# The sticks' values tiles spread over the first attention steps, the gate tiles moved back by three steps

## What is computed

```python
def second_block(x, ...):
    h = rms_norm_2(x, mix_norm_gain)
    proj = h @ w_in
    q_a, k_a, v_a, q_b, k_b, v_b, gate_logits = jnp.split(proj, SPLIT_POINTS, axis=-1)
    y_a = sliding_window_sink_attention(q_a, k_a, v_a, q_gain, k_gain, sinks)   # "windows"
    y_b = stick_breaking_attention(q_b, k_b, v_b)                               # "sticks"
    gates = jax.nn.sigmoid(gate_logits + gate_bias).reshape(b, s, 2, d)
    merged = gates[:, :, 0] * (y_a @ w_up_swa) + gates[:, :, 1] * (y_b @ w_up_sb)
    x = x + merged @ w_out
    h = rms_norm_2(x, ffn_norm_gain)
    return x + peer_ffn(h, peer_w_q, peer_sub_keys, peer_u, peer_v)

def stick_breaking_attention(q, k, v):   # 8 heads of 64, causal, blocks of 128 queries
    z = (q @ k.T) * dh ** -0.5
    log_beta = log_sigmoid(z)
    log_keep = where(before, log_sigmoid(-z), 0)
    suffix = cumsum(log_keep, reverse=True) - log_keep
    return where(before, exp(log_beta + suffix), 0) @ v
```

## Time and profile before

| | us |
|---|---|
| median of 3 runs | 2158.72 |
| lowest and highest of them | 2151.64, 2168.53 |
| the profiled execution, its time | 2159.31 |
| its span | 2158.0 |
| mean granted clock of TensorE in it | 0.985 of full |

### The profile page before, as it was taken

How to read it: one execution, slowest core, us unless ns; L and a number is a source line. 1 busy time by engine, 2 the same in 40 slices (tenths; PEclk the granted TensorE clock), 3 DMA queues, 4 the chain that set the end, 5 groups by cost and what they waited for, 6 DMA issues and landing times.

```text
span 2158.0 us, 36392 instructions
## 1 busy us (share of the span) xinstructions
PE 2096.6 (97%) x14838; PEld 1895.6 (88%) x14838; DVE 1460.1 (68%) x2450; ACT 1054.1 (49%) x1589; POOL 185.8 (9%) x102
## 2 busy tenths in 40 slices
PE   8999999999999999889999899999999999999999
PEld 7997789899889998579988678999999998888887
DVE  5655784766566665856645676899899995555555
ACT  5444633254455444645444875545544445444443
POOL 0000013300010000110004003243000000000000
PEclk9999998999999999899999899999999999999999
DMA  5556221256655555236556335556544446666664
GB/s 199 186 190 209 82 95 60 73 182 195 195 176 177 187 190 182 80 119 196 195 185 203 101 98 188 169 163 187 176 147 147 148 148 195 194 190 191 195 188 153
DMA packets 97637, 352.62 MB, mean 163 GB/s; under 512 B 10896, under 2 KB 12688, under 8 KB 97088
## 3 DMA queue, kind: packets, MB, share of 16 engines
q1 hardware_dynamic: 97472, 350.29, 51.0%
HBM read 349.20 MB, written 1.05 MB: 162 GB/s over the span
## 4 chain that ended last, share of the span: by engine, by line
PE 86%; DVE 8%; ACT 3%; issue 1%; POOL 1%; DMA 0%; SPq 0%; ACTq 0%; DVEq 0%
PE psum L276 26%; PE psum L278 25%; PE psum L277 25%; PE psum L2711 2%; DVE tile_low L205 2%; PE psum L851 1%; ACT tile_high L193 1%; PE psum L347 1%; POOL small L1667 1%; PE psum L1049 1%; PE psum L929 1%; DVE peer_active L2918 0%; ACT hT L490 0%; PE psum L472 0%; PE psum L769 0%
## 5 line engine op out<-in xcount | busy, mean ns | idle before, releaser
L205 DVE TENSOR_TENSOR tile_low<-raw_tiles,tile_high 128x1024 fp32r<-128x1024 f32 x598 | 738.6, 1237 | 508.5 <-ACT tile_high L193 508.2
L193 ACT ACTIVATE tile_high<-raw_tiles 128x1024 fp32r<-128x1024 f32 x642 | 678.2, 1058 | 712.9 <-PE psum L278 708.3
L276 PE MATMUL psum<-hT,tile_high 128*128 128x256 f32 x2560 | 723.5, 283 | 8.8 <-issue 4.7
L277 PE MATMUL psum<-hT,tile_high 128*128 128x256 f32 x2560 | 715.5, 279 | 0.0
L278 PE MATMUL psum<-hT,tile_low 128*128 128x256 f32 x2560 | 715.3, 279 | 0.0
L276 PEld LDWEIGHTS psum<-hT,tile_high 128*128 128x128 f32 x2560 | 486.8, 190 | 10.9 <-issue 7.8
L277 PEld LDWEIGHTS psum<-hT,tile_high 128*128 128x128 f32 x2560 | 484.3, 189 | 0.1
L278 PEld LDWEIGHTS psum<-hT,tile_low 128*128 128x128 f32 x2560 | 483.4, 189 | 0.0
L276 PE MATMUL psum<-tile_high,hT 128*128 128x512 f32 (+1 forms) x816 | 326.1, 400 | 3.3 <-DVE hT L2060 1.6
L278 PE MATMUL psum<-tile_high,hT 128*128 128x512 f32 (+1 forms) x816 | 320.8, 393 | 0.0
L277 PE MATMUL psum<-tile_low,hT 128*128 128x512 f32 (+1 forms) x816 | 318.9, 391 | 0.0
(11 more groups left out here) (357 smaller groups left out, 2226.2 us busy)
## 6 DMA issues: line engine op xcount, KB each, us to landing
raw_tiles<-ffn_in_dram SPq DMA_DIRECT2D x176, 512.0 KB, 3.5
raw_tiles<-peer_u_dram SPq DMA_DIRECT2D x128, 512.0 KB, 3.5
raw_tiles<-peer_v_dram SPq DMA_DIRECT2D x128, 512.0 KB, 3.5
raw_tiles<-ffn_out_dram SPq DMA_DIRECT2D x88, 512.0 KB, 4.3
raw_tiles<-w_kv_dram SPq DMA_DIRECT2D x16, 512.0 KB, 4.2
raw_tiles<-in_gates_dram SPq DMA_DIRECT2D x16, 512.0 KB, 3.5
raw_tiles<-peer_q_dram SPq DMA_DIRECT2D x16, 512.0 KB, 3.8
raw_tiles<-w_k_dram SPq DMA_DIRECT2D x8, 512.0 KB, 3.6
```

What stands on the lines that cost most here:

```text
L193: scalar.activation(k.high[:, n % SLOTS, :], k.raw[:, n % RAW_SLOTS, :], ACT.Copy).then_inc(*k.tile_high_made.mark(n))
L205: vector.tensor_tensor(k.low[:, n % SLOTS, :], k.raw[:, n % RAW_SLOTS, :], k.high[:, n % SLOTS, :].bitcast(F32), ALU.subtract).then_inc(*k ...
L276: k.tensor.matmul(out, still[0], moving[0], start=first, stop=False)
L277: k.tensor.matmul(out, still[0], moving[1], start=False, stop=False)
```

## The change

The values of the sticks become woven tiles like the gates'. Two of their four tiles go ahead of step 0, one each into steps 0 and 1, all into banks 0 and 1. ACT copies their sums at step 2, the first gate group waits for that copy, and PE waits for the emptied banks 0 and 1 ahead of the first values' tile. The gate tiles move to steps 3 to 21 without 7, 12 and 17, the bias to steps 7, 12, 17 and 22. The sticks' turning stays in step 18. The order of the tiles in the stream is the same.

```diff
-GATE_STEPS = [step for step in range(19) if step not in (3, 8, 13)]
+VALUES_AHEAD = 2
+VALUE_STEPS = [0, 1]
+GATE_STEPS = [step for step in range(3, 22) if step not in (7, 12, 17)]
+WOVEN_STEPS = VALUE_STEPS + GATE_STEPS
 BIASED_STEPS = [GATE_STEPS[4 * g + 3] + 1 for g in range(4)]
-STICKS_OUT = GATE_STEPS[-1]
+STICKS_OUT = 18
+MIX2_STEPS = BIASED_STEPS[3] + 1
+def woven_tile(step):
+    return FIRST["in_v_b"][0] + VALUES_AHEAD + WOVEN_STEPS.index(step)
...
-    tensor_tokens(k, "in_v_b", k.hT, k.tokens_copied)
+    def woven(i):
+        g, c0 = i // 4 - 1, 2 * (i % 4)
+        n, pair = take(k)
+        pair = tuple(t.rearrange("p (k n) -> p k n", k=2) for t in pair)
+        for tb in range(TB):
+            if c0 == 0 and g == 0:
+                tensor.wait_ge(*k.tokens_copied.at(("in_v_b", tb, 0)))
+            if c0 == 0 and g > 0:
+                tensor.wait_ge(*k.gates_biased.at((tb, g - 1)))
+            for c in range(2):
+                ins = products(k, k.psum[:, tb, :], part(k.hT, EVERY, c0 + c, block(tb)), part(pair, EVERY, c, EVERY),
+                               c0 + c == 0, c0 + c == KC - 1)
+        ins.then_inc(*k.tile_used.mark(n))
     for b in range(2):
         before, key = k.bank_emptied[b]
         tensor.wait_ge(*before.at(key))
     use_banks(k, range(2, 8))
+    for i in range(VALUES_AHEAD):
+        woven(i)
     tensor.wait_ge(*k.qa_made.at(1))
     tensor.wait_ge(*k.ka_made.at(1))
     tensor.wait_ge(*k.features_out.at(("in_qk_b", 1)))
     tensor.wait_ge(*k.ka_made.at(("in_qk_b", 3)))
-    tensor.wait_ge(*k.tokens_copied.at(("in_v_b", 1, 0)))
...
-    for step in range(units + 4):
+    for step in range(MIX2_STEPS):
...
-        if step in GATE_STEPS:
-            gate(GATE_STEPS.index(step))
+        if step in WOVEN_STEPS:
+            woven(VALUES_AHEAD + WOVEN_STEPS.index(step))
...
-    copied("in_v_b", r["v_b"])
+    def values_copied():
+        for tb in range(TB):
+            scalar.wait_ge(*k.tile_used.at(FIRST["in_v_b"][1] - 1))
+            scalar.activation(r["v_b"][:, tb, :], k.psum[:, tb, :], ACT.Copy, scale=root(k, tb)).then_inc(
+                *k.tokens_copied.mark(("in_v_b", tb, 0)))
...
+    split_high(k, FIRST["in_v_b"][0] + VALUES_AHEAD - 1 + SLOTS)
+    for step in range(MIX2_STEPS):
...
-        if step in GATE_STEPS:
-            split_high(k, gates + GATE_STEPS.index(step) + SLOTS)
+        if step == VALUE_STEPS[-1] + 1:
+            values_copied()
+        if step in WOVEN_STEPS:
+            split_high(k, woven_tile(step) + SLOTS)
...
-    split_low(k, FIRST["in_v_b"][1] - 1 + SLOTS)
+    split_low(k, FIRST["in_v_b"][0] + VALUES_AHEAD - 1 + SLOTS)
...
-        if step in GATE_STEPS:
-            split_low(k, gates + GATE_STEPS.index(step) + SLOTS)
+        if step in WOVEN_STEPS:
+            split_low(k, woven_tile(step) + SLOTS)
```

More of the change, by code:

```diff
@@ L2217, in values @@
         v = r["v_b"] if stick else r["kv_a"]
+        if n == 0:
+            tensor.wait_ge(*k.tokens_copied.at(("in_v_b", 1, 0)))
         ps = bank(k, ("values2", n), k.attended, (2, n))
@@ L2227, in values @@
         ins.then_inc(*k.values_done.mark((2, n)))
[L2229 to L2239, removed]
     units = len(MIX2_UNITS)
@@ L2366, in y_high @@
             turned_high(r["y2"][name][0][:, :, block(tb)], (name, tb), k.y2_turned, (name, tb), k.y2_high_made)
-    gates, up = FIRST["in_gates"][0], FIRST["up_sb"][0]
+    up = FIRST["up_sb"][0]
     units = len(MIX2_UNITS)
-    for step in range(units + 5):
+    split_high(k, FIRST["in_v_b"][0] + VALUES_AHEAD - 1 + SLOTS)
+    for step in range(MIX2_STEPS):
         for late in (6, 5, 4, 3, 2):
```

## The result

| | before | changed |
|---|---|---|
| median of 20 runs, us | 2161.05 | 2164.06 |
| lowest to highest, us | 2151.64 to 2168.53 | 2159.40 to 2171.11 |
| span of the profiled execution, us | 2158.0 | 2167.9 |

The ratio is 1.0023 with a 95% interval of 1.0012 to 1.0034: 2.6 to 7.3 us slower. The forecast was 2157.5 us, 1.2 us faster than the 2158.72 known at that time. Both differences are far under the 1% at which the chances were drawn, but the sign was wrong. The slower rival (a loss of 4.2 us) is nearest.

The account below looks back on a forecast made before the run. TensorE's matmul stream was taken to bound the kernel. From values to up projection, 83.9 us work + 15.9 idle + 5.3 half clock = 105.1 against 106.3, a gain of 1.2: 2157.5 us, own range 2153 to 2161, with rivals 2147 to 2166.

Parts of the forecast that it names:

- The slower rival: Values to up projection: clock falls at every pause, four falls, 10.7 us together; loss 4.2 us, 2162 us; chance 0.25.
- Items 1 to 4: Values' first tile to turning of stick 0: idle 0.85 us for banks, 1.15 for the values' copy, 5.2 before the turning.
- Item 5: Steps 5 and 6: DVE saves the bias's 1.41 us and its wait, and TensorE is not held.
- Item 6: Bias in steps 7, 12, 17 without gate tile: TensorE idles 4.7 us, about 1.1 in step 13, 2.6 in 17 and 18.
- Item 7: Behind step 16: five gate tiles instead of three, all TensorE's time; the up projection's first tile follows at once.
- The sum, its term of half clock: Whole stretch: three clock falls, behind steps 4, 8 and 17, at 5.3 us together.
- my two bounds: Cost of one clock fall, read from slow tiles before the change: 1.7 to 4.2 us.
- Its threshold: The slower rival decides once the clock costs more than 6.5 us in the stretch.
- its sign: First scores to up projection: a granted clock below 0.88 would show the slower rival.
- item 4: Turning of stick 0: 5.2 us idle, passed 7.1 us earlier with two tiles (5.7 us) fewer done; only 1.4 us remain.

Follow-up runs that it names:

- the last experiment: The changed kernel with the bias behind the step's vector work and 72 idle matmuls in pauses: stretch 98.89 us, ratio 0.9972 against the kernel before.
- b2: The kernel before with 36 idle matmuls ahead of the turning of stick 0, nothing else: stretch 101.38 us, ratio 0.9983.

## Why the prediction was wrong

Item by item, with the changed kernel's profile moved by the 5.70 us of its later start.

- *Items 1 to 4, the front: right.* The first tile began 0.82 us late (0.85 forecast). The first scores came at 1184.36 (1184.3 forecast), the first gate tile at 1193.45 (1193.0), the turning of stick 0 at 1201.30 (1201.0) behind 4.85 us (5.2). The copy of the values cost 1.40 (1.15).
- *Item 5, steps 5 and 6: right.* There is no pause in them.
- *Item 6, the bias steps: right in place and size of the pauses.* 4.68 us in steps 7 and 8 (4.7), 1.24 in steps 12 and 13 (1.1), 1.96 in 17 and 18 (2.6). The experiment with the bias behind the vector work shows that the order on DVE makes 2.9 us of them; 2.41 us ahead of the turning of stick 4 and the 1.25 of step 13 stay without it.
- *Item 7, the tail: right that it pays in full, with half clock on top.* It takes 10.85 us more, 5.7 for the two tiles; the rest is 1.96 of pause, which item 6 had, and a clock of 0.86 where it was 1.00.
- *The sum, its term of half clock: this is the step that failed.* Idle time was over-estimated by 1.2 us (15.9 for 14.7). Half clock was taken as three falls at 5.3 us together. There were four. From the lengths of the tiles, transposes, scores and values behind each pause I count about 2.6, 2.1, 1.8 and 2.7, together 9.2 us, and 84.2 for the work, against my 83.9. So 105.1 should have been 83.9 + 14.7 + 9.2 = 107.8, and the profiled stretch is 108.2: the up projection's first product came at 1286.0, not near 1283. Of the 3.9 us that were missing, 1.8 are the fall of step 13, behind 1.24 us of pause, and 2.1 are the size of the other three: 7.4 us where I had put 5.3, close to the lower of my two bounds for each.
- *Why this decided the sign.* The prediction put about 9 us of half clock on the kernel before and 5.3 on the changed one, while it forecast 2.5 us more idle time. The fall of 3.7 us in this term was the whole of the forecast gain, and it did not come. Against the 84.0 us of work of the last experiment, half clock was 8.9 us before and 9.4 changed (means of three executions: 8.4 and 9.0; these are estimates, good to about 1 us). The reason given, that the pauses of 4.93 and 2.02 "each brought one before", left out half of the falls that the trace of before has: that of step 0, behind 1.66 us, and that of step 9, behind 1.33 us.
- *The slower rival* named steps 4, 7 to 8, 13 and 17, and the falls came in 4, 8, 13 and 18. Its threshold, 6.5 us of half clock, was passed; its sign, a clock below 0.88 from the first scores on, was just not reached (0.88). Its name says too much: the pause of 1.40 us in step 3 was followed by a tile of 3.00 us, in all three executions. (Its 2162 us is a slip: 4.2 us above 2158.72 is 2162.9.)
- *The gain of the front and the price of the tail* stand nearly as item 4 said: 6.8 us (7.1 forecast) against 5.7. A margin of 1.4 us cannot carry a forecast of a sign when another term is known only within 8 us. The places and the length of the pauses were right; the size of the clock term was off, and this term held the sign.

The Trainium skill, "TensorE: Matmul & The Clock Gate", section "HAM oscillation — how this bites in real kernels", advises to keep the tiles together ahead of a wait. The runs do not bear that out for the values' tiles: with all four ahead the pause behind them was 7.72 us and the stretch 108.03, about as long as with the tiles spread. The other thought of that section, that the cost of the clock is paid again at each wait, agrees with the runs in part: falls come again and again in the stretch, and filling pauses with idle matmuls took 3.9 us off the changed kernel's stretch; but not every pause brought one.

Open: whether the change costs more than the 1.5 us that the stretches show, as the interval says, and where (with the bias moved, too, the whole time is only 3.0 us below before by its ratio, and the stretch 4.9); whether the two falls that did not come with the bias moved are due to the shorter pauses or to when they came; and what makes a fall come or fail to come behind equal pauses in equal code.

## What to carry to other kernels

Where three engines hand work around in a ring, look for the steps in which TensorE has no filler work. A long job of another engine in such a step shows as a pause of TensorE; in a step that has a filler tile it is covered (the stretch fell from 107.8 to 101.2 us when the steps without a tile were moved away from the bias). Order an engine's queue by who waits next: a bias that nobody needs for one step must not stand ahead of work that the next step turns on (6.6 us of stretch here). Cost a pause of TensorE twice, once for its length and once for the matmuls behind it at half clock, and count the falls that the trace already has before you forecast fewer. If there is nothing useful to put into a pause, idle matmuls into a free bank are worth trying, and their gain has to be measured in place: the same 36 gave 0.8 us in one kernel and about 3.2 in another.

## What the hardware showed that I had not expected

The low level of the clock was seen behind pauses of very different length: 4.93 and 1.66 us in the kernel before (tiles of 3.96 and 4.53 behind them), and 1.24 in step 13 of the changed kernel (3.92). But the length of a pause does not decide it. With the bias moved the same step had a pause of 1.25 us and its tile took 2.88. In step 0 of the kernel before, a pause of 1.66 us was followed by a tile of 4.53 to 4.55 us in three executions and of 2.96 in a fourth (b2, whose edit lies behind it). In step 15 of that kernel, pauses of 2.01 and 2.02 us were followed by tiles of 4.45 and 4.46 us in two executions and of 3.02 in the third. A fall that is avoided can also let another come or go elsewhere: one came in step 5 twice, that of step 9 went once. The three executions of the changed kernel had their falls in the same steps, with tiles of 3.05 to 3.52 us in step 8 and 3.82 to 5.02 in step 13.

One execution therefore can't tell what a change does to the clock: a fall cost 1.5 to 3.2 us here (estimates from the lengths of what ran at the low level), as much as the effects in question.
